# Projection loads moved to another queue, queries turned in place, and the attention output left as lead and remainder

## The reference

```
pz, pzc = h @ w_in, hc @ w_in            # 512 tokens x 1024 -> 2048 q + 512 k + 512 v + 2048 z
q, k = rope_2d(q), rope_2d(k)            # latent tokens only
s  = q @ k.T * HEAD_DIM ** -0.5          # window of 128 keys either side, and all context keys
p  = softmax of s with one sink logit for each head
y  = p @ v
x  = layer_norm(alpha * x  + gate  * ((y * silu(z)) @ w_out))    # latent rows
xc = layer_norm(alpha * xc + gate_c * (...))                     # context rows, the same
```

## Time and profile before

| | us |
|---|---|
| median of 3 runs | 2137.93 (2137.59 to 2150.69) |
| the profiled execution | 2142.43 |
| its span in the profile | 2140.6 |
| mean granted TensorE clock, as a share of full speed | 0.866 |
| PE / DVE / ACT / POOL busy | 1665.9 / 1086.8 / 761.8 / 587.0 |

### The profile page before, as it was taken

One profiled execution on the slowest core, in us unless ns is written; L12 is line 12 of the kernel. 1 busy time (PEld: TensorE's weight loads), 2 busy tenths in 40 slices (PEclk: granted clock), 3 DMA queues, 4 the chain that ended last, 5 costly groups with the idle time before them and its releaser, 6 DMA issues. The chain is left out here.

```text
span 2140.6 us, 27639 instructions
## 1 busy us (share of the span) xinstructions
PE 1665.9 (78%) x10950; PEld 1378.3 (64%) x10950; DVE 1086.8 (51%) x1322; ACT 761.8 (36%) x974; POOL 587.0 (27%) x473
## 2 busy tenths in 40 slices
PE   7849987787696697675665985946699969757998
PEld 1228875666685586565555974735699957347997
DVE  4233422176545447876623546345476643456665
ACT  1221212244411365445243432413345434224543
POOL 0007766577558516886300000000000000000000
PEclk9969998999898798777887997955899989688999
DMA  8746554544432566653666442410454414014541
GB/s 319 285 153 192 189 188 158 217 135 141 170 123 96 169 205 169 169 164 94 175 156 235 158 187 102 155 50 0 158 198 198 172 55 188 5 59 169 206 196 39
DMA packets 135049, 331.78 MB, mean 155 GB/s; under 512 B 31892, under 2 KB 89492, under 8 KB 118820
## 3 DMA queue, kind: packets, MB, share of 16 engines
q1 hardware_dynamic: 128470, 316.64, 43.6%
q10 hardware_dynamic: 6484, 13.85, 1.7%
HBM read 291.80 MB, written 38.65 MB: 154 GB/s over the span
## 5 line engine op out<-in xcount | busy, mean ns | idle before, releaser
L2435 PE MATMUL ffn_ps<-ffn_x_lead,ffn_w_lead 128*128 128x256 f32 x704 | 201.4, 286 | 19.3 <-DVE ffn_x_rest L2506 19.2
L2435 PE MATMUL ffn_ps<-ffn_x_rest,ffn_w_lead 128*128 128x256 f32 x704 | 201.0, 285 | 0.0
L2435 PE MATMUL ffn_ps<-ffn_x_lead,ffn_w_rest 128*128 128x256 f32 x704 | 200.8, 285 | 0.0
L338 PE MATMUL qkvz_ps<-qkvz_w_lead,h_lead 128*128 128x512 f32 x320 | 129.3, 404 | 38.7 <-DVE qkvz_w_rest L271 38.7
L2501 DVE TENSOR_TENSOR ffn_w_rest<-resident_ring,ffn_w_lead 128x2048 fp32r<-128x2048 f32 x44 | 100.7, 2292 | 103.6 <-ACT ffn_w_lead L2470 103.6
L2435 PEld LDWEIGHTS ffn_ps<-ffn_x_lead,ffn_w_lead 128*128 128x128 f32 x704 | 136.9, 194 | 21.0 <-DVE ffn_x_rest L2506 19.9
L2435 PEld LDWEIGHTS ffn_ps<-ffn_x_rest,ffn_w_lead 128*128 128x128 f32 x704 | 137.0, 195 | 0.7
L2435 PEld LDWEIGHTS ffn_ps<-ffn_x_lead,ffn_w_rest 128*128 128x128 f32 x704 | 136.9, 194 | 0.0
L271 DVE TENSOR_TENSOR qkvz_w_rest<-resident_ring,qkvz_w_lead 128x2048 fp32r<-128x2048 f32 x20 | 53.5, 2696 | 159.7 <-ACT qkvz_w_lead L265 155.5
L338 PE MATMUL qkvz_ps<-qkvz_w_rest,h_lead 128*128 128x512 f32 x320 | 128.4, 401 | 0.0
L338 PE MATMUL qkvz_ps<-qkvz_w_lead,h_rest 128*128 128x512 f32 x320 | 128.2, 401 | 0.0
(11 more groups left out here) (428 smaller groups left out, 4650.1 us busy)
## 6 DMA issues: line engine op xcount, KB each, us to landing
resident_ring<-in_ffn_gu SPq DMA_DIRECT2D x22, 2048.0 KB, 9.1
resident_ring<-in_ada_w SPq DMA_DIRECT2D x12, 2048.0 KB, 7.7
ffn_wd<-in_ffn_down SPq DMA_DIRECT2D x22, 1024.0 KB, 4.9
resident_ring<-in_attn_w_in SPq DMA_DIRECT2D x10, 2048.0 KB, 11.2
xc<-s_q_scratch SPq DMA_DIRECT2D x128, 128.0 KB
resident_x<-in_s_bT SPq DMA_DIRECT2D x64, 256.0 KB
s_W_scratch<-resident_x SPq DMA_DIRECT2D x64, 256.0 KB, 2.7
resident_ring<-in_w_out SPq DMA_DIRECT2D x8, 2048.0 KB, 8.2
```

Source lines behind the costliest of these rows:

```text
L338: last = nc.tensor.matmul(bank(parity, t), self.lhs[x][:, half * HK + k, t * P:(t + 1) * P], self.w[w][:, j, k, :], start=(half, k, x, w) ...
L2435: last = nc.tensor.matmul(ps[s][f][:, m, :], w_part[w][:, m, k, f * P:(f + 1) * P], x_part[x][:, k, :], start=(k, w, x) == (0, 0, 0), stop ...
```

## The change

- **Projection.** The loads of the weight tiles are issued by ACT instead of SP. In the body of group g ACT makes lead 0 of group g + 1, waits for the rests of group g, issues the load of tile g + 2 (for g = 8, 9 the first two tiles of `w_out`), and makes lead 1 of group g + 1. SP has only its 36 turns.
- **Weights of the later stage.** `turn(n)` loads block n + 3 instead of n + 2, in the projection and in the attention.
- **Queries.** The tile `qs` and POOL's 16 copies are gone; PE transposes the queries straight from `q`. For that, PE's steps are written out instead of looped.
- **Outputs.** ACT's copy of the transposed output goes to `y_lead` in fp32r (same place in its order). DVE has one instruction more in a step, for each of 16 heads: `ps_t` minus `y_lead` into `y_rest`, which lies over the head's queries in `q`. It stands behind `maxima(i+1)` and ahead of the copies of the probabilities. The next user of `ps_t` on PE waits for it: `turn_queries(i+2)`, from head 4 on, and `turn_outputs`.
- **Output projection.** It multiplies `y_lead` and `y_rest` as they are; the four `x_lead` and four `x_rest` pieces are gone.

The diff, cut to its core:

```
@@ -214,13 +214,14 @@
-    def __init__(self, core, ph, groups, halves, ntt, mm_done, src=None, lhs=None):
+    def __init__(self, core, ph, groups, halves, ntt, mm_done, src=None, lhs=None, at=None):
         self.core, self.groups, self.halves, self.ntt, self.mm_done, self.src = core, groups, halves, ntt, mm_done, src
         self.lhs = lhs
+        self.at = at if at is not None else lambda x, k, t: self.lhs[x][:, k, t * P:(t + 1) * P]
         self.lead_made, self.rest_made, self.x_lead_made, self.x_rest_made = [ph.sem(n) for n in ("lead_made", "rest_made", "x_lead_made", "x_rest_made")]
@@ -335,7 +336,7 @@
                         for x, w in ((0, 0), (0, 1), (1, 0)):
-                            last = nc.tensor.matmul(bank(parity, t), self.lhs[x][:, half * HK + k, t * P:(t + 1) * P], self.w[w][:, j, k, :],
+                            last = nc.tensor.matmul(bank(parity, t), self.at(x, half * HK + k, t), self.w[w][:, j, k, :],
                                                     start=(half, k, x, w) == (0, 0, 0, 0),
@@ -536,15 +537,8 @@
                 weights.begin(sp)
-                done = 0
-                for u in range(2, NT):
-                    sp.wait_ge(split.rest_made, 2 * (u - 1))
-                    core.load(sp, u % 2, d["attn_w_in"][u])
-                    upto = W_QKVZ * (u - 1) // (NT - 2)
-                    for n in range(done, upto):
-                        weights.turn(sp, n)
-                    done = upto
-                split.following(sp, d["w_out0"])
+                for n in range(W_QKVZ):
+                    weights.turn(sp, n)
                 weights.last(sp)
@@ -564,14 +558,18 @@
                 def empty(g, s, dst, tiles, func):
-                    split.ahead_scalar(act, g, s, isinstance(g, int) and g == NT - 1)
+                    if g < NT - 1:
+                        split.lead(act, g + 1, 1 - s, 0, 0)
+                    act.wait_ge(split.rest_made, 2 * (g + 1))
+                    core.load(act, s, d["attn_w_in"][g + 2] if g < NT - 2 else d["w_out0"][g + 2 - NT])
+                    if g < NT - 1:
+                        split.lead(act, g + 1, 1 - s, 0, 1)
                     for t in tiles:
-                with act.Fori(0, 2) as i:
-                    for s in range(2):
-                        empty(i * 2 + s, s, lambda t: q[:, t, bass.ts(i * 2 + s, NW)], (2, 3), ACT.Copy)
+                for g in range(4):
+                    empty(g, g % 2, lambda t: q[:, t, g * NW:(g + 1) * NW], (2, 3), ACT.Copy)
                 empty(4, 0, lambda t: kn[:, t, :], (2, 3), ACT.Copy)
@@ -631,8 +629,7 @@
         p_sb = work[:, 3:6, :]
-        qs = work[:, 6, :]
-        qT = work[:, 7, :]
+        qT = work[:, 6, :]
         pT = [ph.sb(f"pT{s}", [P, 3, NW]) for s in range(2)]
@@ -646,26 +643,15 @@
         ps_y = ph.ps("ps_y", [P, TT, HD])
-        names = ["qs_ready", "q_turned", "qT_ready", "scores_ready", "max_ready", "exp_ready", "p_turned",
-                 "pT_act", "pT_dve", "pv_ready", "yz_ready", "yz_turned", "yzT_ready", "k_turned", "kT_ready",
+        names = ["q_turned", "qT_ready", "scores_ready", "max_ready", "exp_ready", "p_turned",
+                 "pT_act", "pT_dve", "pv_ready", "yz_ready", "yz_turned", "yzT_ready", "y_rest_made", "k_turned", "kT_ready",
                  "loads", "steps"]
-        (qs_ready, q_turned, qT_ready, scores_ready, max_ready, exp_ready, p_turned, pT_act, pT_dve, pv_ready,
-         yz_ready, yz_turned, yzT_ready, k_turned, kT_ready, loads, steps) = [ph.sem(n) for n in names]
+        (q_turned, qT_ready, scores_ready, max_ready, exp_ready, p_turned, pT_act, pT_dve, pv_ready,
+         yz_ready, yz_turned, yzT_ready, y_rest_made, k_turned, kT_ready, loads, steps) = [ph.sem(n) for n in names]
         ident = core.ident
-        def schedule(eng, step):
-            for i in (-1, 0, 1):
-                step(i, i % 2)
-            turns = (NH - 4) // 2
-            with eng.Fori(0, turns) as n:
-                for s in range(2):
-                    step(n * 2 + 2 + s, s)
-            for i in range(2 + 2 * turns, NH + 2):
-                step(i, i % 2)
         def exists(i, shift=0):
@@ -673,14 +659,8 @@
             def _(pool):
-                heads = lambda h: nc.gpsimd.tensor_copy(qs.rearrange("p (t w) -> p t w", t=TT), q[:, :, bass.ts(h, HD)]).then_inc(qs_ready, 1)
-                heads(0)
-                for h in range(NH):
-                    if h + 1 < NH:
-                        pool.wait_ge(q_turned, h + 1)
-                        heads(h + 1)
-                    for n in range(weights.blocks * h // NH, weights.blocks * (h + 1) // NH):
-                        weights.make(pool, n)
+                for n in range(weights.blocks):
+                    weights.make(pool, n)
@@ -699,11 +679,11 @@
                 def turn_queries(h):
-                    pe.wait_ge(qs_ready, h + 1)
                     pe.wait_ge(qT_ready, h + 1)
-                    pe.wait_ge(yzT_ready, h + 1)
+                    if h >= 4:
+                        pe.wait_ge(y_rest_made, h - 3)
                     for t in range(TT):
-                        last = nc.tensor.transpose(ps_t[:, t * P:(t + 1) * P], qs[:, t * P:(t + 1) * P], ident[:])
+                        last = nc.tensor.transpose(ps_t[:, t * P:(t + 1) * P], q[:, t, h * HD:(h + 1) * HD], ident[:])
                     last.then_inc(q_turned, 1)
@@ -741,7 +721,8 @@
                     pe.wait_ge(yz_ready, h + 2)
-                    pe.wait_ge(yzT_ready, h + 4)
+                    if h:
+                        pe.wait_ge(y_rest_made, h)
                     pe.wait_ge(qT_ready, min(h + 5, NH + 1) if isinstance(h, int) else h + 5)
@@ -765,7 +746,8 @@
                         mix(i - 1, 1 - s)
-                schedule(pe, step)
+                for i in range(-1, NH + 2):
+                    step(i, i % 2)
@@ -773,7 +755,6 @@
                 prime(act, qT_ready, 1)
-                prime(act, yzT_ready, 4)
                 for g in range(KVH):
@@ -795,7 +776,7 @@
                         act.wait_ge(yz_turned, i)
-                        nc.scalar.activation(yzT[:, i - 2, :], ps_t[:], ACT.Copy).then_inc(yzT_ready, 1)
+                        nc.scalar.activation(y_lead[:, i - 2, :], ps_t[:], ACT.Copy).then_inc(yzT_ready, 1)
                     if exists(i):
@@ -837,6 +818,10 @@
                         maxima(i + 1)
+                    if exists(i, -2):
+                        dve.wait_ge(yzT_ready, i - 1)
+                        tiles = lambda m: m.rearrange("p (t w) -> p t w", t=TT)
+                        nc.vector.tensor_tensor(y_rest(i - 2), tiles(ps_t[:]), tiles(y_lead[:, i - 2, :].bitcast(F32)), ALU.subtract).then_inc(y_rest_made, 1)
                     if exists(i):
@@ -884,7 +869,7 @@
         mm_done, rows_ready, steps, var_ready, std_ready, ready = [ph.sem(x) for x in names]
-        split = Split(core, ph, 2, 2, n, mm_done, src=yzT)
+        split = Split(core, ph, 2, 2, n, mm_done, src=yzT, at=parts_at)
         quads = EarlyQuads(core, ph) if early else None
@@ -1183,8 +1168,8 @@
         self.store(sp, n)
-        if 2 <= n < self.blocks - 2:
-            self.load(sp, n + 2)
+        if 1 <= n < self.blocks - 3:
+            self.load(sp, n + 3)
@@ -2567,22 +2552,26 @@
                 context = [(xc[:, t, :], 1) for t in range(LT)]
-                with ExitStack() as heads, ExitStack() as outputs:
-                    q, z = [within(heads, n, [P, TT, E], side="right") for n in "qz"]
+                with ExitStack() as kept, ExitStack() as heads, ExitStack() as outputs:
+                    q = within(kept, "q", [P, TT, E], side="right")
+                    y_low = nc.alloc_sbuf_tensor_at("y_rest", [P, TT, E], F32R, offset=nc.sbuf_top)
+                    z = within(heads, "z", [P, TT, E], side="right")
                     kn, v = [within(heads, n, [P, TT, KVW], side="right") for n in ("kn", "v")]
                         attention_projection(core, hparts, q, kn, v, z, xc)
-                    yzT = within(outputs, "yzT", [P, ET, NTOK])
+                    y_lead = within(outputs, "y_lead", [P, ET, NTOK], F32R)
+                    y_rest = lambda h, t=slice(0, TT): y_low[:, t, h * HD:(h + 1) * HD]
+                    y_parts = lambda x, k, t: y_rest(k, t) if x else y_lead[:, k, t * P:(t + 1) * P]
                     with ExitStack() as inner:
-                        kT, work = within(inner, "kT", [P, KVH, NTOK]), within(inner, "work", [P, KT, NTOK])
-                        attention(core, q, kn, v, z, kT, work, yzT, xc)
+                        kT, work = within(inner, "kT", [P, KVH, NTOK]), within(inner, "work", [P, KT - 1, NTOK])
+                        attention(core, q, kn, v, z, kT, work, y_lead, y_rest, xc)
                     heads.close()
                     rows_of = lambda m: m.rearrange("(t p) n -> p t n", p=P)
```

(8 more changed lines are left out.)

2 lines of the change are left out of this document (1 added, 1 removed).

## The result

The changed kernel takes 2157.89 us (median of 12 executions, 2146.57 to 2161.60), the kernel before 2139.89 in the same runs (12 executions, 2133.85 to 2150.69): 1.007 of before, interval 1.0054 to 1.0087. It is slower, by less than 1%; the forecast was 2135 and slightly faster. The time lies at the upper end of the range of 2112 to 2158, on the other side of the kernel before. The profiled execution took 2160.26 us with a span of 2158.4, 17.8 longer than before.

A forecast was written before the change was run, and what follows sets the result against it. It took PE as the bound, held by late weight tiles in the projection and POOL's query copies in the attention; -33.4 + 16.0 + 1.4 + 15.1 - 2.3 = -3.2 us gave a forecast of 2135 us, range 2112 to 2158.

The forecast's parts named there:

- the term for the clock, +15.1: Attention: PE's clock falls after 7 of 12 waits of 3.18 us, at 2.15 us each, +15.1 us.
- Projection, -33.4: Projection: at 21.78 us a group, PE's last group ends at 377.9 instead of 411.34, -33.4 us.
- the tiles are late because of the order on SP: Projection: weight-tile loads stand behind 4 or 5 of SP's waits for POOL's blocks; SP's queue waits 246.2 us.
- condition (c): Projection: POOL must end before PE; at least 27 of its 69 us of waits go, else 27 us are lost.
- All three conditions: Projection: tiles land within 26 us, ACT has time for the issue and its new wait, POOL ends before PE.
- The wait for the subtraction: Attention: PE waits 3.18 us for DVE's 0.69 us subtraction in every step, making a step 10.84 us.
- Rival 4: Attention: PE does not wait for DVE; twelve steps take 91.9 us, sum -57.9, 2080 us; chance 0.10.
- Rival 2: Attention: the clock falls in every wait; +7.5 at the mean price, +15.4 at the dearer, 2145 to 2153 us; chance 0.17.
- Last heads and output projection, +1.4 - 2.3: Two more waits for a subtraction in the last heads, +1.4; output projection starts without the `x_rest` between, -2.3 us.
- the twelve steps without their falls: Attention, scores of head 3 to head 15: 12 x 10.84 = 130.1 us instead of 114.14, +16.0 us.

The follow-up runs named there:

- x10: Kernel before with only the projection's weight-tile loads issued by ACT instead of SP; 2143.88 us, 1.0036 of before.
- x13: Kernel before with only the look-ahead: POOL's blocks loaded three ahead instead of two; 2081.08 us, 0.9734 of before.
- x14: Changed kernel with the weight-tile loads back on SP between its turns; 2160.42 us, 1.0103 of before.
- x4: Changed kernel plus 24 useless transposes of the identity on PE ahead of each wait for `y_rest` from head 4 on; 2128.79 us, 0.9947 of before.
- x3: Changed kernel with DVE's subtraction moved forward, behind the work on the first tile of the scores; 2091.26 us, 0.9765 of before.
- x5: Changed kernel without the outputs part, keeping queries from `q`, tile loads on ACT and blocks three ahead; 2085.33 us, 0.975 of before.
- x6: Changed kernel, but ACT copies `ps_t` twice into SBUF and DVE subtracts from there at its step's end; 2090.35 us, 0.9771 of before.
- x1: Changed kernel with DVE's subtraction moved forward, between the two reductions of the maxima; 2119.42 us, 0.9898 of before.
- x2: Changed kernel with DVE's subtraction moved forward, ahead of both reductions of the maxima; 2104.92 us, 0.9816 of before.
- x8: Kernel before with only the queries turned straight from `q`, without POOL's copies; 2142.09 us, 1.0004 of before.
- x12: Changed kernel plus 2 useless transposes of the identity on PE ahead of each wait for `y_rest`; 2147.33 us, 1.0048 of before.
- x11: Changed kernel with blocks loaded two ahead again instead of three; 2207.97 us, 1.0334 of before.

## Why the prediction was wrong

The step that turned a small gain into a loss is the term for the clock, +15.1: 7 falls at 2.15 us, where the runs showed 11 at 2.70, 29.7 us. With that in its place the prediction's own sum is +11.4 and not -3.2. The other terms, and the causes behind them:

- **Projection, -33.4:** right in size (411.34 to 378.88, -32.5), but the gain was put down to the wrong part of the change. The reading of the earlier trace rows as "the tiles are late because of the order on SP" holds for PE: x10 changes this order alone, and PE's last product is done at 375.39. POOL then ended the stage, at 411.02. SP's queue waited 154.2 us for POOL in the projection (the 246.2 of the earlier trace rows hold the attention too), and POOL waited 69.4 for loads that SP issued one block too late. The look-ahead breaks this circle for PE and for POOL, and x13 has the whole gain with it alone. I had the needed number in condition (c), "at least 27 of the 69 go", as a proviso for a gain of another part. All three conditions held: tiles landed in 10.0 us by the median, ACT's new wait delayed nothing, and 50.5 of the 69.4 us went, so that POOL's last block was done 12 us before PE. The size came from PE's own pace and holds whichever part frees PE and POOL, so the right number says nothing for the cause.
- **A rule that I set aside fits the times, but not the waits.** The Trainium skill, DMA: Bandwidth & Descriptors, section Issuing engines are not separate DMA queues, has issue from several engines save only issuing time. I answered that here SP's wait for POOL was saved as well. By x10 and x14 the tiles on ACT are worth nothing in the program's time. But x10 shows more saved than issuing time: PE was through with the projection 36 us earlier, and only POOL's end hid it.
- **The wait for the subtraction:** right. 3.17 us in the profile against 3.18; 10.82 for the step without a fall (x4) against 10.84; 0.68 for the subtraction against 0.69. Rival 4, a PE that does not wait for DVE, is not this kernel; x3, x5 and x6 come near it, with 2085 to 2091 us against its 2080.
- **The clock, +15.1: the term that failed.** I took 7 falls of 12 at 2.15 us. There were 11 at 2.70, 29.7 us. The rows on either side of 3.18 did not decide it, as I said; but I took half for a wait that returns with the same length in each step. Once the transposes themselves were in the fall, the step repeated itself at 13.6 us. Why it locks so is open; the runs show only that it does at 3.17 us and not at 2.4 (x1). Rival 2 is what happened, with the dearer price: its 2153 us against the 2157.9 measured. The trace agrees with the Trainium skill, TensorE: Matmul & The Clock Gate, section HAM oscillation — how this bites in real kernels: a wait for data in every turn of the loop, and a fall in nearly every turn. It is not so for every length of the wait: x2 waits 1.3 us in every turn and has no fall.
- **Start of the attention:** a term that was missing. From the last product to the scores of head 3 it took 31.27 us at a granted clock of 0.84, before 29.12 at 0.94: +2.15. The transposes of k are among what ran at 1.2 GHz (16 in 2.73 us).
- **Last heads and output projection, +1.4 - 2.3:** together +1.3 instead of -0.9. The last heads took 2.2 more, not 1.4. PE waits 10.97 us for the first rest instead of 11.90, so 0.9 of the 2.3 came: no `x_rest` stands between, but ACT began the first lead of the weights 7.34 us after PE's last transpose, before 5.98.

The misses add up: 14.6 (clock) + 0.9 (projection) + 2.2 (start) + 2.2 (last heads and output projection) + 1.4 (behind) is 21.3; less 0.3 for the twelve steps without their falls (129.85 for 130.1), that is the 21.0 between -3.2 and +17.8.

## What to carry to other kernels

Where two engines end a stage within a few us of each other, as PE and POOL did here, price each part of a change against both: a part that speeds up one alone shows nothing (x8, x10), and the part that frees both, here the look-ahead, gets the whole gain. When an instruction must read a bank that the next work needs, put it as early in its engine's step as its data allow, or copy the bank out and read the copy; here that place decided between 2158 and 2091 us. A wait of some 3 us in each turn of a loop on PE costs the wait and a fall of the clock beside it, so cost it at both.

## What the runs showed of the hardware

Waits that differ little had very different prices in this loop: with one of 1.3 us in each step the clock fell in none of 12 steps (x2), at 2.4 us in 2 (x1), at 2.95 in 5 (x12), at 3.17 in 11 (the kernel after), 12 (x11) and 10 (x14); each is one profiled execution. A fall cost 1.5 us (x1), 1.63 (behind the four transposes) or 2.8 (transposes and all of `mix` slow). Useless transposes, 24 in a step, made the program 29 us faster (2157.89 to 2128.79): the wait's path stayed the same, and only the falls behind it were gone.
